# Two small inverse square roots moved from ScalarE and VectorE to a power on GpSimd, in a fused RWKV-7 block

## The reference

```python
kk = heads(k * k_k)
kk = kk / jnp.maximum(jnp.linalg.norm(kk, axis=-1, keepdims=True), 1e-12)
k = k * (1 + (a - 1) * k_a)
o = wkv7_scan(rh, heads(decay), kh, vh, kk, heads(a))
o = layer_norm(o, gn_g..., gn_b..., GN_EPS)      # per head: (o - mu) * rsqrt(var + eps)
```

## Time and profile before

| | |
|---|---|
| median of 3 runs | 1051.26 us |
| profiled execution | 1055.53 us, its span 1053.8 us, mean granted TensorE clock 0.974 |
| TensorE matmul busy | 969.4 us, 92% |
| VectorE busy | 677.1 us, 64% |
| ScalarE busy | 474.3 us, 45% |
| GpSimd busy | 381.2 us, 36% |
| chain that ended last | TensorE 74%, VectorE 15%, ScalarE 3%, issue 3%, DMA 2%, GpSimd 2%, SyncE's queue 1% |

### The profile page before, as it was taken

How to read it: one execution, slowest core, us unless ns; L and a number is a source line. 1 busy time by engine, 2 the same in 40 slices (tenths; PEclk the granted TensorE clock), 3 DMA queues, 4 the chain that set the end, 5 groups by cost and what they waited for, 6 DMA issues and landing times.

```text
span 1053.8 us, 27460 instructions
## 1 busy us (share of the span) xinstructions
PE 969.4 (92%) x11539; PEld 806.5 (77%) x11539; DVE 677.1 (64%) x925; ACT 474.3 (45%) x579; POOL 381.2 (36%) x222
## 2 busy tenths in 40 slices
PE   1998889999989999899899999798999999999993
PEld 1776677777768678667688888688899898998993
DVE  7325567668837867664222255468778788787887
ACT  0546344346435633434532242274545446455451
POOL 8332510411240131123554445245153352451542
PEclk9998998999999999999999999889999999999997
DMA  9332234234332333332344337222341442423201
GB/s 362 119 98 68 81 87 141 55 91 124 93 82 84 96 96 101 103 109 61 121 120 110 107 112 230 70 61 81 94 146 40 120 119 60 139 80 97 63 1 81
DMA packets 122967, 108.10 MB, mean 103 GB/s; under 512 B 5411, under 2 KB 104657, under 8 KB 122865
## 3 DMA queue, kind: packets, MB, share of 16 engines
q1 hardware_dynamic: 112768, 83.44, 26.4%
q10 hardware_dynamic: 10097, 23.16, 7.2%
HBM read 100.23 MB, written 2.10 MB: 97 GB/s over the span
## 4 chain that ended last, share of the span: by engine, by line
PE 74%; DVE 15%; ACT 3%; issue 3%; DMA 2%; POOL 2%; SPq 1%; ACTq 0%; DVEq 0%; POOLq 0%
PE set L2247 13%; PE bank L1882 11%; PE bank L2333 7%; PE set L2333 7%; PE set L2186 6%; PE bank L2186 5%; PE set L1936 4%; PE set L2285 3%; PE bank L2247 2%; PE set L1924 2%; PE set L1948 2%; PE bank L1863 2%; DVE y L1502 1%; PE set L1960 1%; DVE Q L1276 1%
## 5 line engine op out<-in xcount | busy, mean ns | idle before, releaser
L663 POOL TENSOR_TENSOR w_lo<-w_raw,w_hi 128x1024 fp32r<-128x1024 f32 (+2 forms) x75 | 171.2, 2282 | 388.0 <-ACT w_hi L773 379.4
L773 ACT ACTIVATE w_hi<-w_raw 128x1024 fp32r<-128x1024 f32 (+2 forms) x81 | 81.8, 1010 | 103.9 <-PE set L2186 35.2
L822 ACT ACTIVATE Q<-set 128x1024 f32<-128x1024 f32 x56 | 57.5, 1026 | 134.4 <-PE set L1936 68.9
L1882 PE MATMUL bank<-h_hi,w_hi 128*128 128x512 f32 x256 | 108.7, 425 | 3.4 <-POOL w_lo L663 3.3
L1152 ACT ACTIVATE w_hi<-w_raw 128x1024 fp32r<-128x1024 f32 x70 | 74.3, 1062 | 81.2 <-PE set L2247 64.3
L1614 DVE SCALAR_TENSOR_TENSOR res<-set,mod,res 128x256 f32<-128x256 f32 x192 | 92.9, 484 | 25.2 <-PE set L2247 16.5
L2247 PE MATMUL set<-a_hi,w_hi 128*128 128x256 f32 x384 | 108.9, 284 | 0.0
L2247 PE MATMUL set<-a_hi,w_lo 128*128 128x256 f32 x384 | 108.6, 283 | 0.0
L2247 PE MATMUL set<-a_lo,w_hi 128*128 128x256 f32 x384 | 108.6, 283 | 0.0
L1882 PE MATMUL bank<-h_lo,w_hi 128*128 128x512 f32 x256 | 104.2, 407 | 0.2 <-issue 0.2
L1882 PE MATMUL bank<-h_hi,w_lo 128*128 128x512 f32 x256 | 103.6, 405 | 0.0
(11 more groups left out here) (361 smaller groups left out, 2322.8 us busy)
## 6 DMA issues: line engine op xcount, KB each, us to landing
w_raw<-in_w_ff_dram SPq DMA_DIRECT2D x64, 512.0 KB, 3.9
w_raw<-in_w_in_dram SPq DMA_DIRECT2D x46, 512.0 KB, 3.7
y<-in_w_ada_dram ACTq DMA_DIRECT2D x20, 512.0 KB, 3.7
ada<-in_w_ada_dram SPq DMA_DIRECT2D x16, 512.0 KB, 10.3
Q<-in_w_ada_dram ACTq DMA_DIRECT2D x12, 512.0 KB, 3.7
w_raw<-in_w_rwkv_up_dram SPq DMA_DIRECT2D x8, 512.0 KB, 3.6
w_raw<-in_w_out_dram SPq DMA_DIRECT2D x8, 512.0 KB, 4.5
xtok<-in_x_dram SPq DMA_DIRECT2D x4, 512.0 KB, 6.7
```

What stands on the lines that cost most here:

```text
L663: link(pool.tensor_tensor(part_of(k, w_lo), raw_part(k), part_of(k, w_hi).bitcast(F32), ALU.subtract), "lo_ready")
L773: link(act.activation(part_of(k, w_hi), raw_part(k), ACT.Copy), "hi_ready")
L822: link(act.activation(by_half(tile), psum_flat(set_of(name)), ACT.Copy), "act_kept")
L1882: mm = pe.matmul(o, w, hx, start=(m == 0), stop=(m == 3 * KT - 1))
```

## The change

The roots on ScalarE and the reciprocals on VectorE go. For the key norms VectorE reads the sums out of PSUM itself, with a maximum of 1e-24 on the squared norm (`squared_norms`, slots 5 and 14), and GpSimd raises the 128x8 numbers to the power -1/2 (`inverse_norms`, slots 5 and 13). For the group norm GpSimd raises the 128x16 variances (slot 10; slot 2 in the last turn). The exponent comes from a tile of constants.

```diff
+            link(pool.memset(minus_half[:, :], -0.5))
...
+            def inverse_norms(it, q):
+                m = 2 * (it + 1) + q
+                pool.wait_ge(sem("norm_taken"), m + 1)
+                if m:
+                    pool.wait_ge(sem("inverse_taken"), m)
+                link(pool.tensor_tensor(inverse[:, :], norms[:, :], minus_half[:, 0:2 * TB], ALU.pow), "inverse_ready")
+
             def slot(it, s):
...
+                if n < QUADS and s in (5, 13):
+                    inverse_norms(it, s // 13)
+                if 1 <= it < QUADS and s == 10 or it == QUADS and s == 2:
+                    pool.wait_ge(sem("o_var"), it)
+                    link(pool.tensor_tensor(gn[:, 3, :], gn[:, 1, :], minus_half[:, :], ALU.pow), "o_root")
...
-            def norm_root(it, q):
-                m = 2 * (it + 1) + q
-                wait_made(act, f"norm{q}", it)
-                if m:
-                    act.wait_ge(sem("inverse_ready"), m)
-                link(act.activation(norms[:, :], pset[set_of(f"norm{q}")][:, 0, 0:2 * TB], ACT.Sqrt), "norm_taken")
...
-                if s == 9 and tail and it < QUADS:
-                    act.wait_ge(sem("o_var"), it)
-                    link(act.activation(gn[:, 2, :], gn[:, 1, :], ACT.Sqrt), "o_std")
...
-            def norm_inverse(n, q):
-                dve.wait_ge(sem("norm_taken"), 2 * n + q + 1)
-                link(dve.tensor_scalar(norms[:, :], norms[:, :], 1e-12, None, ALU.max))
+            def squared_norms(n, q):
+                wait_made(dve, f"norm{q}", n - 1)
                 if 2 * n + q:
-                    dve.wait_ge(sem("inverse_taken"), 2 * n + q)
-                link(dve.reciprocal(inverse[:, :], norms[:, :]), "inverse_ready")
+                    dve.wait_ge(sem("inverse_ready"), 2 * n + q)
+                link(dve.tensor_scalar(norms[:, :], pset[set_of(f"norm{q}")][:, 0, 0:2 * TB], 1e-24, None, ALU.max), "norm_taken")
...
-                        dve.wait_ge(sem("o_std"), it)
-                        link(dve.reciprocal(gn[:, 3, :], gn[:, 2, :]))
+                        dve.wait_ge(sem("o_root"), it)
                         link(dve.tensor_tensor(blocks16(O), blocks16(O), gn[:, 3, :].unsqueeze(2).to_broadcast([P, 16, N]), ALU.mult), "o_normed")
```

More of the change, by code:

```diff
@@ L101, in build @@
         rec = sb("rec", [P, 16])
+        minus_half = sb("minus_half", [P, 16])
         gn = sb("gn", [P, 4, 16])
@@ L922, in slot @@
                     keep_pair(b1, b2, "AP0", it)
-                if s == 14 and prep:
-                    norm_root(it, 1)
                 k = landing(it, s)
@@ L953, in slot @@
                         keep(b5, "A2T", it)
-                if s == 5:
-                    if prep:
-                        norm_root(it, 0)
                 if s == 6 and work:
@@ L1018, in slot @@
                         y_high(m)
-                if it == QUADS and s == 2:
-                    act.wait_ge(sem("o_var"), it)
-                    link(act.activation(gn[:, 2, :], gn[:, 1, :], ACT.Sqrt), "o_std")
                 if work and s in ADA_LOADED and s != 12:
@@ L1414, in slot @@
                         decay_sums(n, 0)
+                if s == 5 and prep:
+                    squared_norms(n, 0)
                 if s == 6:
@@ L1418, in slot @@
                         keep_plus_one(b4, "A4T", "A4I", it)
-                    if prep:
-                        norm_inverse(n, 0)
                 if s == 7:
@@ L1455, in slot @@
                     if prep:
-                        norm_inverse(n, 1)
+                        squared_norms(n, 1)
                     if tail:
```

## The result

| | before | after |
|---|---|---|
| median | 1051.87 us (4 runs) | 1072.74 us (4 runs, 1070.22 to 1075.48) |
| profiled execution, its span | 1055.53, 1053.8 us | 1073.03, 1071.3 us |
| mean granted clock of it | 0.974 | 0.968 |
| ratio | | 1.0211, 95% interval 1.0182 to 1.0241 |

The changed kernel is 20.9 us slower. The forecast was 1048.9 us with a range of 1043.5 to 1064, so the result lies outside the range, on the side of rival 1, the dear power, which had 0.24 of the chances, 0.07 of them for "far above 1068".

What follows compares the result with a forecast made beforehand. TensorE, busy 92% of the span, bounds the kernel; its waits between 76 and 520 us hold 15.7 us. Terms 5.9 - 0.65 - 1.8 - 0.4 - 0.7 = 2.4 us won, 1051.26 to 1048.9 us; range 1043.5 to 1064.

Steps and rivals of the forecast that it cites:

- rival 1: All powers: each costs as much as a large subtraction, 2.34 us, giving 1058.8 us, or 1068 at 4.7; chance 0.24.
- I take the middle rows: Price of a GpSimd power: 0.74 us for 8 numbers, 1.31 for 16, chosen between bounds from subtractions.
- clock term: Turn -1, behind the first stop: full clock instead of 0.68 for 5.3 us, 1.7 us won.
- (b): Turns 1 to 3, before yT: the power holds VectorE's two-input step, 0.64 us lost, against 0.28 saved by a reciprocal.
- steps for the two norms: Turn -1: first key norm gains 2.0 us at the low part, second gains 0.95 us at TensorE's longest such stop.
- rival 3: Turn -1: only the first power is slow; 1050.6 us and the delay, about 1056 by the skill page; chance 0.08.
- rival 4: ScalarE: Square or Copy want their own table, so it isn't freed and only losses stay, 1054 us; chance 0.03.
- The third term: Turn -1, second wait for a low part: VectorE's preparation comes some 5 us earlier, gain 1.3 us.
- Turn 0: Second key norm, late through VectorE's maximum: the power then delays TensorE, a loss of 0.65 us.
- (a): Turns 1 and 2: VectorE releases the norm's set late, D1 waits 0.8 us, 0.36 is taken back, loss 0.5.
- (c): Turns 1 and 2: the 2.5 us Tanh wait goes, but TensorE waits for VectorE at yT instead and wins nothing.
- Turn 3 and 4: Turn 3 loses 0.4 us by VectorE's held step; turn 4 loses 0.7 as the power delays y_low and a transfer.

Runs made afterwards that it cites:

- row_cheap: Changed kernel with its constants in row 2 of gn and a product in place of each power: 1054.0 us, ratio 1.0019.
- row: Changed kernel with its constants in the free row 2 of gn, so no tile moves: 1070.4 us, ratio 1.0166.
- pad: Kernel before with an unused tile ahead of gn, so later tiles lie 64 bytes further on: 1055.0 us, ratio 1.0013.
- copy: Kernel before with a copy in place of each of ScalarE's twelve roots, so 24 table loads go: 1051.7 us, ratio 0.9995.
- all_early: Changed kernel, constants in gn, key maxima, modulations and group product reordered, last power behind three y_low, unread root in turns 1 and 2: 1052.2 us, ratio 1.0004.

## Why the prediction was wrong

**The price** (the step "I take the middle rows") is the term that failed with the largest size. I put a power at 0.74 and 1.31 us; it took 1.64 and 2.90, 2.2 times as much. The bounds, 0.19 to 2.34 and 0.2 to 4.7, held; the choice inside them did not, and it had no row to rest on. Of the 22.1 us of GpSimd time between row_cheap and row, 13.6 were not in the forecast (0.9 for each of 8 powers, 1.59 for each of 4), and by the 16.4 us that the whole cost I estimate 10 us for them, stops and clock together. The rival for a dear power had the slope nearly right: "some 10 us lost for each us of the price" against 16.4 / 1.42 = 11.5 measured between row_cheap and row. With the measured prices my own steps give: turn -1 wins 1.56 + 0.05 + 1.3 without its clock term, 2.9 us; turn 0 loses 1.55, turns 1 and 2 2.49 each, turn 3 1.99, turn 4 2.29, in sum 7.9 us of work lost. Measured in row: 4.3. Of the 3.6 between, 1.9 are the lock of (b), three times 0.64.

**Turn -1** went as its steps for the two norms say, once the price is put in. The chain of the kernel after (it answers to the earlier trace rows):

```profile
78.54 1.66 POOL L682 TENSOR_TENSOR inverse<-norms,minus_half 128x8 f32<-128x8 f32 x1 [6.27 <-DVE norms L1310]
80.28 2.36 POOL L665 TENSOR_TENSOR w_lo<-w_raw,w_hi 128x1024 fp32r<-128x1024 f32 x1
82.69 0.50 PE L1875 MATMUL bank<-h_hi,w_hi 128*128 128x512 f32 x1 [0.66 <-POOL w_lo L665]
...
95.33 1.12 PE L1994 MATMUL set<-ident,inverse 128*64 128x128 f32 x8 [2.09 <-POOL inverse L682]
```

The low part stands behind the power, as I said it would, and TensorE waits 0.66 us for it in place of 1.99; the second stop is 2.09 us in place of 2.11, where my sum with 1.64 us gives a gain of 0.05. The first power is no slower than the others (1.66 us), so rival 3 is out, and rival 4 with the 24 loads that are gone. The clock behind the first stop was 1.00 from 82.69 to 88.00 us, as forecast, but that gain is no sure one: pad has the old stop of 1.99 us and 1.00 behind it too. The third term, 1.3 us from the second low part, was mis-sized: everything came 4 us earlier, TensorE with it, and the stop is 0.81 us in place of 1.27, in copy 1.27 still.

**Turn 0** measured as the price alone says: 3.47 us against 1.94, a loss of 1.53; 0.65 + 0.9 = 1.55 by my step. Only the price was wrong here.

**Turns 1 and 2, (a)** was right: `D1` waits 0.8 us in each. **(b), the lock, was wrong.** Turn 1 of the kernel after, GpSimd and VectorE (it answers to the earlier trace rows):

```profile
252.87 2.90 POOL L691 TENSOR_TENSOR gn<-gn,minus_half 128x16 f32<-128x16 f32 x1 [2.04 <-DVE gn L1433]
...
253.55 0.75 DVE L1332 SCALAR_TENSOR_TENSOR G<-G,params,t 128x512 f32<-128x512 f32 x1
255.87 1.23 DVE L1439 TENSOR_TENSOR O<-O,gn 128x1024 f32<-128x1024 f32 x1 [0.45 <-POOL gn L691]
```

The step with two inputs, which I had held for the power's whole length, ran for its normal 0.75 us inside the power. The Trainium skill (SBUF — State Buffer, SBUF: two separate sides) has the shared ports locked for a whole instruction; the power is an instruction by which this trace disagrees, while for low parts it agrees. What VectorE paid is only 0.45 us of waiting. The other way round a power was held: two of the eight key powers took 2.62 us, both starting 0.1 us behind a two-input VectorE step of 1.22 us.

**(c) is the step whose mechanism failed.** I wrote that the Tanh stop goes, that TensorE waits at `yT` instead, and "wins nothing". As work this is right to 0.2 us: 1.26 + 0.86 became 2.34 in copy. But I counted the clock only where a stop vanished (1.7 us won in turn -1) and nowhere that a stop grew or two became one. The merged stop costs 2.6 us of clock on average in each of the two turns, 5.3 together, and this is the size of what eats copy's gain. In row_cheap too, where the power costs nothing, lost clock time is 5.3 us over the kernel before. In row it is 14.3: the other 9 come with the price. The profile that I had showed both sides: stops of 1.26 and 0.86 us at full clock and a dip behind 1.99.

**Turn 3 and 4.** In turn 3 VectorE waited 2.2 us for the power, where it had waited 0.8 for the root, and the `yT` stop grew from 2.3 to 3.4, against the 0.4 forecast. In turn 4 I named one chain, from the power through `y_low` and the low part to the transfer, and it is there; I overlooked the modulations behind the product in VectorE's list, on which TensorE waits as well. The question "who is queued behind the waiting instruction" was asked of GpSimd's list and not of VectorE's. "ScalarE's two loads there save nothing" was wrong as well: in copy, without them, TensorE's wait for the pooling weights is 0.45 us in place of 1.83. From 490 to 530 us after's matmuls fell behind before's by 5.8 us, against the 0.7 forecast.

**The addresses**, 4.1 us, were in no step and no rival: a constant tile was costed at nothing.

The gain from the freed ScalarE was right in size by luck: 4.2 us of work by my steps for turn -1, 5.0 in copy, where the two norms give 2.5, the second low part nothing, and the rest comes elsewhere, 1.4 of it in turn 4. So of the 23.3 us between the change that was forecast (2.4 won) and the one measured (20.9 lost) about 4 are addresses, 13 are clock (11 lost, where the forecast had 1.7 won), and the other 6 are stops and steps. By cause instead of by measure, the price is the largest part, some 10 us of stops and clock, and the merged stops are some 5.

Three smaller slips stand in the prediction. The 15.7 us of the earlier trace rows were called all that can be won besides clock, but TensorE stood 12.6 us more under "issue" in that stretch. At 2.34 us for 16, turn 3 loses 1.4 and not 1.2. And rival 4's "losses alone" add up to 3.5 us, 1054.8 and not 1054.

## What to carry to other kernels

Where the busiest engine stops, ask not only how long but in how many pieces: an engine set free can merge two stops that the clock survives into one that it doesn't, and here useless work that kept them apart was worth 2 to 4 us. Split times into span times clock and the rest before explaining a few per cent. When a change adds a tile, put it where it moves no other, and when it adds a wait, read what is queued behind it on *both* engines.

## What the runs showed of the hardware

- A power on GpSimd, float32, took 1.64 us for 128x8 and 2.90 us for 128x16 numbers, by estimate 0.16 us for each number of a row and 0.38 fixed; products took 0.20 and 0.22 us.
- A power on GpSimd didn't hold a two-input VectorE step that began inside it (0.75 us inside 2.90). A subtraction of 128x1024 did (1.97 in place of 0.75), and `y_low`, of 128x512, also stretched VectorE steps on 128x8 with one input: three took 2.30 us beside it and 0.58 without.
- The other way round, a power of 128x8 that began 0.1 us behind a two-input VectorE step was stretched: to 2.62 us behind a step of 1.22 us (after), to 2.68 behind one of 1.28 (all_early).
- 64 bytes more ahead of the tiles stretched some matmuls from 227 to as much as 241 ns from start to start, 4 us in 1050. The cause is open.
- A stop of TensorE of 2.05 to 2.50 us in one piece was followed by half clock in 20 of 22 cases; stops of 1.26 and of 0.58 to 1.01 us, 4 us apart, in 1 of 18. A stop of 2.13 to 3.43 us in turn 3 was followed by none in 6 of 20.
